# Moving the token table, the one-hot rows and half of a held weight piece in a mixture-of-experts decoder layer

## The reference

```python
hn = rms_norm(h, norm_ffn_l)
h = h + moe_ffn(hn.reshape(-1, D_MODEL), *moe_w).reshape(h.shape)
# in moe_ffn:
p_grp = softmax(h @ w_rg + b_rg); grp = argmax(p_grp)         # the group of each token
w2, e_loc = lax.top_k(softmax(le_g), TOP_K)                   # two experts in it, with weights
slot_tok = jnp.full((P,), N).at[dest].set(tok_sorted)         # which token sits in which slot
xb = h_pad[slot_tok].reshape(n_blk, EXPERT_BLOCK, D)          # rows gathered by expert
y = (silu(xe @ w_g[e]) * (xe @ w_u[e])) @ w_d[e]              # three matrices an expert, 6 MB
```

## Time and profile before

| | us |
|---|---|
| median of 3 runs | 905.92 (903.79 to 905.94) |
| the profiled execution | 907.63 |
| its span, first to last instruction | 905.7 |
| TensorE busy | 888.5 (98% of the span) |
| VectorE busy | 656.8 (73%) |
| ScalarE busy | 204.3 (23%) |
| GpSimd busy | 70.1 (8%) |

### The profile page before, as it was taken

How to read it: one execution, slowest core, us unless ns; L and a number is a source line. 1 busy time by engine, 2 the same in 40 slices (tenths; PEclk the granted TensorE clock), 3 DMA queues, 4 the chain that set the end, 5 groups by cost and what they waited for, 6 DMA issues and landing times.

```text
span 905.7 us, 11854 instructions
## 1 busy us (share of the span) xinstructions
PE 888.5 (98%) x4539; PEld 464.1 (51%) x4539; DVE 656.8 (73%) x1290; ACT 204.3 (23%) x475; POOL 70.1 (8%) x72
## 2 busy tenths in 40 slices
PE   8999999999999999999999999999999999999998
PEld 7866998776544446444333433334434333333544
DVE  6568986668767764565867768678687686757895
ACT  4122231018645204411111111111111111111411
POOL 4021061000000000110000000000000000000000
PEclk9999999999999999999999999999999999999999
DMA  9752835530008776899999999999999999999502
GB/s 302 221 200 71 248 98 173 185 123 1 1 1 194 287 268 228 314 380 422 416 428 426 425 424 427 425 424 425 427 420 423 420 422 421 420 423 379 215 24 76
DMA packets 70269, 262.83 MB, mean 290 GB/s; under 512 B 11882, under 2 KB 38006, under 8 KB 53412
## 3 DMA queue, kind: packets, MB, share of 16 engines
q1 hardware_dynamic: 64864, 250.73, 70.9%
q0 software_dynamic: 4080, 8.93, 2.9%
q10 hardware_dynamic: 1268, 2.40, 0.7%
HBM read 254.95 MB, written 13.08 MB: 296 GB/s over the span
## 4 chain that ended last, share of the span: by engine, by line
PE 82%; DMA 9%; DVE 4%; SPq 3%; ACT 1%; issue 1%; POOLq 0%; DVEq 0%; ACTq 0%
PE ps L1451 75%; DMA w<-in_w_exp_down 4%; DMA w<-in_w_exp_up 4%; SPq L522 3%; PE ps L1946 2%; PE ps L2233 1%; PE ps L1475 1%; DMA h<-in_x_prompt 1%; PE ps L2274 1%; DMA xg<-hn_rows,sidx 1%; PE ps L1486 0%; PE ps L1949 0%; PE ps L1749 0%; PE ps L1639 0%; DVE probs L3098 0%
## 5 line engine op out<-in xcount | busy, mean ns | idle before, releaser
L1451 PE MATMUL ps<-w,xe 128*64 128x512 f32 x1024 | 228.1, 596 | 3.6 <-DMA w<-in_w_exp_up 3.5
L3516 DVE TENSOR_TENSOR h<-h,ps 128x1024 f32<-128x1024 f32 x120 | 143.2, 1215 | 104.6 <-PE ps L1451 104.5
L1451 PEld LDWEIGHTS ps<-w,xe 128*64 128x64 f32 x1024 | 70.1, 137 | 142.8 <-issue 134.1
L1451 PE MATMUL ps<-w,hT 128*64 128x512 f32 x504 | 115.4, 599 | 2.0 <-DMA w<-in_w_exp_down 2.0
L1451 PE MATMUL ps<-yk,ST 128*128 128x512 f32 (+1 forms) x320 | 105.2, 431 | 0.1
L1392 ACT ACTIVATE sg<-ps 64x256 f32<-64x256 f32 x64 | 24.1, 377 | 245.0 <-PE ps L1451 244.6
L984 POOL DMA_INDIRECT xg<-hn_rows,sidx x32 | 31.9, 998 | 611.7 <-PE ps L2233 375.3
L1451 PEld LDWEIGHTS ps<-yk,ST 128*128 128x128 f32 (+1 forms) x320 | 48.5, 174 | 56.3 <-issue 27.2
L1403 ACT ACTIVATE yk<-ps 64x512 fp32r<-64x512 f32 x64 | 38.0, 593 | 148.2 <-PE ps L1451 147.4
L1451 PEld LDWEIGHTS ps<-w,hT 128*64 128x64 f32 x504 | 33.3, 136 | 69.2 <-issue 69.0
L1451 PE MATMUL ps<-xT,wring 128*128 128x272 f32 x192 | 54.0, 408 | 0.0
(11 more groups left out here) (478 smaller groups left out, 1216.1 us busy)
## 6 DMA issues: line engine op xcount, KB each, us to landing
w<-in_w_exp_down SPq DMA_DIRECT2D x27, 2048.0 KB, 28.2
w<-in_w_exp_gate SPq DMA_DIRECT2D x32, 1024.0 KB, 30.3
w<-in_w_exp_up SPq DMA_DIRECT2D x32, 1024.0 KB, 31.1
w<-in_w_exp_gate SPq DMA_DIRECT2D x14, 2048.0 KB, 17.4
w<-in_w_exp_up SPq DMA_DIRECT2D x14, 2048.0 KB, 22.4
w<-in_w_exp_down SPq DMA_DIRECT2D x9, 1024.0 KB, 12.1
wring<-in_w_in SPq DMA_DIRECT2D x12, 512.0 KB, 6.8
h<-in_x_prompt SPq DMA_DIRECT2D x8, 512.0 KB, 6.0
```

The source lines that it names most:

```text
L1451: return nc.tensor.matmul(out, l, r, start=start, stop=stop, skip_group_check=skip)
L3516: TTn(h[0:r, t, :], h[0:r, t, :], both(b, r), ALU.add).then_inc(S["hadd"], 1)
```

## The change

- `R` is placed at 72.25 to 74.75 KB, where `hotS` was, instead of at `free2`.
- `hotS` is placed at 76 to 78.5 KB, where the first gather lands and where `hnt[1]` staged the rows of tile 3 before. So VectorE now waits for all five writes of normed rows (`hn_out`, 16 x 5) before it writes `hotS`.
- `early[0]` no longer shares its place with `R`; its load is issued after `product_done(3)`, and the wait for `sl_ps` in SP's order is gone with it.

```diff
-        hotS = at("hotS", [P, 2 * TT, SLOTS], 72.25 * K)
+        hotS = at("hotS", [P, 2 * TT, SLOTS], 76 * K)
+        R = at("R", [P, 2 * TT, 2, NE], 72.25 * K)
...
-        R = at("R", [P, 2 * TT, 2, NE], free2)
...
             sp.wait_ge(S["op_done"], product_done(3))
+            sp.dma_start(early[0][:], held[:, 0:1024]).then_inc(S[f"wc{CC - 1}"], 16)
             sp.wait_ge(S["op_h"], upto("w12", "w2", "w1"))
...
             embed_out(5, 1, 0, D)
-            sp.wait_ge(S["sl_ps"], 1)
-            sp.dma_start(early[0][:], held[:, 0:1024]).then_inc(S[f"wc{CC - 1}"], 16)
             embed_out(6, 2, 0, D)
...
             chain(V.reduce_sum(sin[:], lt[:], axis=X))
+            dve.wait_ge(S["hn_out"], 16 * TT)
             for k in range(2):
                 TTn(hotS[:, k * TT:(k + 1) * TT, :], ...
```

## The result

The changed kernel takes 907.56 us in the median of 14 executions (905.35 to 910.35), the kernel before 905.68 (903.79 to 907.02) beside it. The ratio is 1.0029, with a 95% interval of 1.0020 to 1.0038: about 1.9 us slower. The forecast was 907.7 us, and its sum of 1.8 us came out nearly exactly. Its reasons did not: two of its terms were wrong in opposite directions, so the closeness of the number is luck. In all that follows the ratio is the recorded one, of executions beside each other; it isn't the quotient of the two medians and can differ from it by 0.002. One execution of the kernel before took 3159 us in a later session and is left out of the ratios.

The account below looks back on a forecast made before the run. Bound: a steady weight stream whose start hangs on TensorE and the first gather. Wait 2.13 us less 0.3 for the gather gave 1.8, so 905.92 + 1.8 = 907.7 us; own range 906.5 to 908.3, 8-in-10 range 905.3 to 909.2.

Parts of the forecast that it names:

- What bounds the kernel: Expert stage: a steady weight stream whose start hangs on TensorE and the first gather; lateness at 382.8 us is paid in full.
- The new wait, 2.13 us: VectorE before `hotS`: idle from 373.70 until the last normed rows land at 375.83, moving the gather and kernel by 2.13 us.
- The held piece taken from the gather's side, 0.3 us: First gather: without the 0.52 MB load moving beside it, it lands 0.3 us sooner.
- The estimate from the Trainium skill's fit: First gather: would land in 3.6 us, at 383.2, making the sum 0.65 instead of 1.8 us.
- The upper bound that I gave: First gather: at most 1.43 of the 2.13 us can come back, as TensorE isn't free before 383.52.
- TensorE's own work, to end at 383.52: TensorE ahead of the gathered rows: its work ends at 383.52 instead of 381.39 us.
- TensorE idle 2 us more before the slot sums: Router's end: sign of a right forecast, TensorE standing idle 2 us longer before the slot sums.
- the wide one: Whole kernel: the 8-in-10 range of the time, 905.3 to 909.2 us.
- The covered wait: VectorE before `hotS`: last rows land by 373.7, so the wait costs nothing; 905.6 to 905.9 us; chance 0.10.
- The shortened stream: Expert weight stream: 0.52 MB moved out from before it saves 1.2 us, 905.4 or 904.4 us; chance 0.08.
- The rows that land later still: Last write of normed rows: lands up to 1.3 us later, costing 3.4 us in all, 909.3 us; chance 0.16.
- The early gather: First gather: lands early without the held piece, sum 0.65 us, 906.6 us; included in the main forecast's chance of 0.66.

Follow-up runs that it names:

- the short matmuls: Changed kernel with three unread 128x256 matmuls put ahead of the slot sums; 906.20 us against 905.48 for the kernel before, ratio 1.0003.
- the third experiment: Kernel before with only the held piece's 512 KB load put after the last write of embedding rows; 907.94 us against 906.66, ratio 1.0007.

## Why the prediction came out right, and where it was wrong

*What bounds the kernel.* Right. The stage of the experts is a stream of fixed length, and its start hangs on TensorE: the 445.2 us of the table hold for starts from 382.4 to 388.9 us. It also held that the stream gets no shorter with 0.52 MB gone from before it: 445.22 in the changed kernel.

*The new wait, 2.13 us.* The mechanism, the place and what stands behind it were right. As a number it was that of one execution: 0.97, 0.99, 1.12, 1.43, 1.69, 2.04, 2.44 and 2.46 us in the eight profiles with the wait, 1.64 on average. The 9.0 us for the last row write were not a property of that write. In the kernel before that I predicted from, the write of tile 1 had landed quickly (5.6 us from 357.12), so that tile 2 was copied at 364.01; in the changed profile it took 8.6 us, tile 2 was copied at 364.87, and the last write came later and landed sooner (6.2). The other profiles show the same pattern: where tile 1's write landed in 4.7 to 6.5 us the last one took 9.0 to 9.2, elsewhere 6.1 to 7.8. I should have given the wait a range.

*The held piece taken from the gather's side, 0.3 us.* This step failed: the term was mis-sized. The gather's landing fell from 5.3 to 2.8 us, and what came back was all of TensorE's wait for it: the variants without the wait are 1.55 and 1.77 us shorter from RT to FE. I had sized the dependence by a gather among full queues at 402 us (5.9), and took from 5.9 against 5.3 that load hardly matters. But both were loaded: the two rows lay on the same side, and no row showed an unloaded gather. The estimate from the Trainium skill's fit ("DMA: Bandwidth & Descriptors", "Anatomy of one DMA"), 3.6 us, which I set aside as not borne out, was the nearer one; its 2.6 us without the GpSimd part that I had added was nearer still. The upper bound that I gave, 1.43 us back until TensorE's own work ends, is what happened: at the forecast's wait and at full clock the sum would be 0.5 to 0.65 us.

*TensorE's own work, to end at 383.52.* It ended at 383.34, but for another reason than the 2.13 us of waiting: 1.3 us of idle time and 1.6 us at half clock, in an execution that had begun 1.05 us earlier. The clock is the term that I left out, and the second step that failed. I noted "TensorE idle 2 us more before the slot sums" as a sign to look for and gave it no price, since the clock of the kernel before was full everywhere, behind gaps of the same length too (1.48 us at 382.87 and 2.04 at 829.98). The gap isn't enough to make a fall certain, but in the changed kernel 18 of 26 executions had a low clock, against 16 of 98 of the kernel before.

So the sum should read: 0.4 to 0.6 us without the clock, and +1.3 for the falls on average. The first is the difference of the executions at 0.999 or 1.0. The second is the difference of (1 - mean clock) times the span between the two kernels where both were measured beside each other (1.89 against 0.56 us), as rough as that measure is. Together 1.7 to 1.9, where 1.9 and 2.0 were measured. The first part, taken apart, is the wait less the 1.6 or 1.7 us that the early gather gives back: that was +0.7 at a wait of 2.46 (the short matmuls), but -0.4 in the changed kernel's own two profiles, with waits of 1.12 and 1.43, once their falls are taken off. How long the wait is in its other executions isn't known, so this part is shown in direction and bound, not in size. The forecast had +2.1 and -0.3 instead, and no falls: too much for the wait, too little for the gather, nothing for the clock, and the errors cancelled. Without the falls the change would be within what can be measured; its 906.1 to 906.3 us would have lain below the forecast's own range (906.5 to 908.3), and inside the wide one.

*The rivals.* The covered wait: no profile with the wait had less than 0.97 us. The shortened stream: no. The rows that land later still: they landed up to 0.3 us later than in the profile of before, and the price of 3.4 us that this rival had is reached in single executions (910.35), through the clock and not through the landing. The early gather, given as the lower end, was right as a mechanism, as the third experiment shows.

## What to carry to other kernels

Placing a tensor where it needs a new wait can undo what the freed place gives: the same change with `hotS` in two odd corners and no wait is 0.1% faster than before (just about measurable), with the wait 0.3% slower. Price an idle gap on the matrix engine by more than its length, and where the order lets work be put into the gap, do that first: swapping two steps took 2.0 us off the same stage, most of it by the fall that didn't come. To size how a transfer depends on load, look for a row without load; two loaded rows say nothing about it, and then the bound of the next engine's own work is the end of the range to take seriously.

## What the runs showed of the hardware

- TensorE's granted clock fell to 0.50 behind idle gaps of 1.3 to 2.4 us of TensorE, in a stretch in which it had been busy throughout but for the gap, and stayed there for 3.4 us in most profiles and 6.8 us in two (behind gaps of 1.97 and 2.37 us). Gaps of 1.5 and 2.0 us also passed without a fall. A fall of 3.4 us costs 1.6 to 1.7.
- An indirect gather of 128 rows of 2 KB landed in 2.7 to 2.9 us, also with a 512 KB write issued 0.6 us before it. It took 3.3 us behind a 512 KB load issued 1.4 us before it, 5.3 behind such a write and such a load issued 0.6 and 0.25 us before it, and 5.9 to 9.9 in the stream.
- In the one profile of it, 512 KB put right ahead of a saturated stream lengthened it by 2.1 us, where its bytes at 421 GB/s are 1.2.
